# Paged attention in a two-layer decoder step: one more latent page of each unit loaded instead of turned by TensorE

## The chip, the cores and the metric

The kernel runs on one core of one Trainium2 chip. The metric is the device time of one execution in microseconds; the value of a kernel is the median of its runs. The engines are TensorE (PE; its weight loads are listed as PEld), VectorE (DVE), ScalarE (ACT), GpSimd (POOL) and SyncE (SP). A name with a q behind it (ACTq, SPq) is an engine's instruction queue: register work and DMA issues.

## The reference, cut to what matters

One inference step of a small decoder with two layers, for a new prompt of 256 tokens and for 8 samples of 8 new tokens each. The first layer has a gated delta rule mixer, the second latent attention; around each mixer stand two half-step SwiGLU blocks of width 2816. The model width is 1024, everything is float32. What the change touches is the attention of the second layer:

```python
kc  = concatenate([cache_ckv[page_table], c_new])      # latents, 256 wide
kpe = concatenate([cache_kpe[page_table], pe_new])     # rotary keys, 64 wide
s = (q_lat . kc + q_pe . kpe) * scale                   # 8 heads
p = softmax(where(k_pos <= q_pos, s, -inf))
o_lat = p . kc                                          # the same kc as keys and as values
```

A sample has 2048 past tokens in 16 pages of 128 tokens, at places that the page table gives. The latent is both key and value. The scores need a page with the latent's features on the partitions, the values need it with the page's keys on the partitions.

## The kernel before, in words

Weights come in chunks of 1 MB, which ScalarE and VectorE split into a high and a low part (lines 221 to 236); each matmul by weights is three passes of these parts. All of that before and behind the attention is dense work of TensorE. The attention proper starts at 1090 us of the span and ends at 1225 us.

**Units.** The samples are taken in four pairs (NP = 4). A pair's 16 pages go in four quads of QP = 4 pages (NQT = 4), so there are NUN = 16 units; unit i is quad i % 4 of pair i // 4. A unit handles four pages of each of the pair's two samples: the first sample (s = 0) on 64 partitions of the scores, the second (s = 1) on the other 64. Beside it runs one of the 16 pieces of the prompt's own attention (8 heads by 2 query tiles, PU; an even unit has a short piece with one key tile, an odd unit a long one with two). Each iteration n of the loop in attention_pe (line 2308) is, on TensorE:

1. scores_pe(n): 24 matmuls (lines 2240 and 2244) on the feature-major pages in one of three slots;
2. new_values_pe in unit 1, and numerators_pe(n - 1) (line 2256): four transposes of the last unit's exponentials;
3. in units 1, 5, 9 new_scores_pe (lines 2185 to 2187), for the pair's new tokens; then page_plain_pe(n) (line 2267): transposes of pages of the first sample; in units 3, 7, 11 new_transposed_pe (line 2191), in units 4, 8, 12 new_values_pe (line 2195);
4. p_numerators_pe(n) (line 2109): one or two transposes of the prompt's normalized probabilities;
5. values_pe(n - 1) (line 2284): 16 instructions on key-major pages, two for each page, which counts pv_page up by one;
6. p_values_pe(n) and p_scores_pe(n + 1) (lines 2117 and 2098 to 2101), and behind a pair's last values outputs_pe (line 2292).

**Key-major pages.** For the second sample (plain_b) all four come by DMA from cache_c, two by SyncE and two by GpSimd (load_plain, line 2523). For the first sample, pages 2 and 3 come by DMA from ScalarE's queue (plain_c, load_first_plain, line 2512). Pages 0 and 1 are turned by TensorE: page_plain_pe transposes two 128x128 halves of each, out of the feature-major slot, into PSUM bank 6 (C_BANK[0]), and VectorE's copy_plain (line 2409) brings them into plain_a, for all units the same buffer. So it waits until the values of the unit before have read it.

**ScalarE's order** is written out by hand (attention_act, line 2334). In iteration n: the prompt's exponential p_exp_act(n) (line 2124); transposed(n - 1) (line 2348), the copy of the transposed numerators to SBUF for which values_pe waits; numerators(n) (line 2339), the unit's exponential, which waits for VectorE's row maximum; new_exp_act in units 2, 6, 10 (line 2199); p_transposed_act(n) (line 2132), for which p_values_pe waits; p_high_act(n) (line 2139), the copy of the prompt piece's output; then load_first_plain(n + 1); and in units 4, 8, 12 high (line 2353), the copy of a finished pair's output. Each load there is a page number read from SBUF (page_of, line 2500), register work, and the DMA's issue (line 2520).

**VectorE's order** (attention_dve, line 2395): p_mask_dve (lines 2150 to 2155), p_norm_dve (lines 2161 and 2163), which waits for p_exp_act, row_max (lines 2398 to 2403), copy_plain, merge (lines 2417 and 2421), and in units 4, 8, 12 norm, p_low_dve (line 2169) and low (line 2437).

SyncE and GpSimd load the feature-major slots (load_pages, line 2502), each one sample of the pair; the load for unit i waits for c_tr, which page_plain_pe(i - 3) counts up at its end.

Of the kernel before, what the change touches and what calls it, by code (L numbers as in the profile page):

```python
# [27 lines left out]
P = 128  # L28
D_MODEL, SEQ, DEC_B, DEC_S = 1024, 256, 8, 8
FFN_DIM, HEADS, CONV_W = 2816, 8, 4  # L30
PAST, PAGE, KV_LORA, ROPE, NOPE, Q_LORA = 2048, 128, 256, 64, 128, 512
# [18 lines left out]
BASE, NCHUNK = {}, 0  # L50
# [62 lines left out]
def build(nc, io):  # L113
    ctx = ExitStack()
    with ctx:
        def sb(name, shape, dt=F32, where=ctx):
            return where.enter_context(nc.sbuf_tensor(name, shape, dt))


        def sem(name):  # L120
            return ctx.enter_context(nc.semaphore(name))


        raw = [sb(f"raw{i}", [P, CHUNK]) for i in range(2)]
# [10 lines left out]
        ssum = sb("ssum", [P, TOK])  # L135
# [6 lines left out]
        r_pre = sb("r_pre", [P, TOK])  # L142
# [4 lines left out]
        ident = con[:, 0:P]  # L147
# [33 lines left out]
        bank = [psum[:, i, :] for i in range(8)]  # L181
# [1665 lines left out]
        def kv_pool(pool):  # L1847
# [6 lines left out]
        QP = 4  # L1854
# [6 lines left out]
        NTS = 3  # L1861
# [3 lines left out]
        slot = [u.rearrange("p (g s n) -> p g s n", g=QP, s=2) for u in uoff]  # L1865
        qd = marena[:, o_:o_ + 4 * TOK].rearrange("p (t n) -> p t n", t=4)
        o_ += UW
        plain_a = marena[:, o_:o_ + CW_ // 2].rearrange("p (g c) -> p g c", g=QP)
        plain_b = [[raw[BASE["uk"] % 2][:, 1536 + g * KV_LORA:1536 + (g + 1) * KV_LORA] for g in range(2)]
                   + [raw[(BASE["uk"] + 1) % 2][:, 1280 + g * KV_LORA:1280 + (g + 1) * KV_LORA] for g in range(2)],  # L1870
                   [marena[:, o_ + CW_ // 2 + g * KV_LORA:o_ + CW_ // 2 + (g + 1) * KV_LORA] for g in range(QP)]]
        plain_c = [[plain_a[:, 2, :], plain_a[:, 3, :]],
                   [raw[(BASE["uk"] + 1) % 2][:, 1792:1792 + KV_LORA], r_pre[:, 0:KV_LORA]]]
        o_ += CW_
        qpe = marena[:, o_:o_ + HEADS // 2 * TOK].rearrange("p (h t) -> p h t", h=HEADS // 2)
        assert 2 * UW <= H2 and o_ + HEADS * TOK <= AW - H2 - 2 * 2 * HEADS * TOK
# [36 lines left out]
        qland = [qland, sem("plain_landed1")]  # L1913
# [173 lines left out]
        S_BANK, PS_BANK, PP_BANK, PO_BANK, T_BANK, V_BANK, C_BANK = 0, 2, 3, 3, 4, 5, (6, 7)  # L2087
# [130 lines left out]
        def new_acc_dve(dve, p):  # L2218
            dve.wait_ge(n_pv, p + 1)
            dve.tensor_copy(oacc[p], new_bank(KV_LORA)).then_inc(n_acc, 1)  # L2220
# [38 lines left out]
        def page_plain_pe(pe, i):  # L2259
            if i:  # L2260
                pe.wait_ge(c_dve, i)
            if i % NQT == 1 and i > NQT:
                pe.wait_ge(s_lo, 2 * (i // NQT))
            for g in range(2):
                for w in range(2):
                    o = (2 * g + w) * P
                    last = pe.transpose(bank[C_BANK[0]][:, o:o + P], slot[i % NTS][:, g, 0, w * P:(w + 1) * P], ident)
            last.then_inc(c_tr, 1)

        def first_plain(i, g):  # L2270
            return plain_a[:, g, :] if g < 2 else plain_c[i % 2][g - 2]

        def values_pe(pe, i):
            pe.wait_ge(s_trt, i + 1)
            pe.wait_ge(c_dve, i + 1)
            pe.wait_ge(qland[i % 2], 16 * 2 * (i // 2 + 1))
            pe.wait_ge(spland[i % 2], 16 * 2 * (i // 2 + 1))
            pe.wait_ge(ppland[i % 2], 16 * 2 * (i // 2 + 1))
            if i:
                pe.wait_ge(s_o, i)  # L2280
            for g in range(QP):
                for s in range(2):
                    rows = slice(s * NSMP, (s + 1) * NSMP)
                    last = pe.matmul(bank[V_BANK][rows, 0:KV_LORA], pts[:, g, rows], plain_b[i % 2][g] if s else first_plain(i, g),  # L2284
                                     start=(g == 0), stop=(g == QP - 1))
                last.then_inc(pv_page, 1)
# [101 lines left out]
        def olv(a, p, c):  # L2388
            t0 = SEQ + 2 * DEC_S * p
            return a[:, c:2 * HEADS:2, t0:t0 + 2 * DEC_S].rearrange("p h (s t) -> p s h t", s=2)  # L2390

        def obank(c):
            return bank[C_BANK[0]][:, c * P:(c + 1) * P].rearrange("p (s h t) -> p s h t", s=2, h=HEADS)

        def attention_dve(dve):
            def row_max(i):
                dve.wait_ge(s_done, i + 1)
                dve.tensor_reduce(ust(i, 0), psum[:, S_BANK:S_BANK + 2, 0:QP * HP], AX.XY, ALU.max).then_inc(s_mx, 1)
                dve.wait_ge(s_mx, 3 * i + 1)
                old = ust(i - 1, 1) if i % NQT else nst(0, i // NQT)  # L2400
                dve.tensor_tensor(ust(i, 1), ust(i, 0), old, ALU.max).then_inc(s_mx, 1)
                dve.wait_ge(s_mx, 3 * i + 2)
                dve.tensor_scalar(ust(i, 2), ust(i, 1), -SCALE, None, ALU.mult).then_inc(s_mx, 1)

            def copy_plain(i):
                dve.wait_ge(c_tr, i + 1)
                if i:
                    dve.wait_ge(pv_page, QP * (i - 1) + 2)
                dve.tensor_copy(plain_a[:, 0:2, :], bank[C_BANK[0]][:, :].rearrange("p (g c) -> p g c", g=2)).then_inc(c_dve, 1)

            def merge(i):
                p = i // NQT
                dve.wait_ge(s_alpha, i + 1)
                if i % NQT:
                    dve.wait_ge(s_l, i)
                old = ust(i - 1, 5) if i % NQT else nst(2, p)
                dve.scalar_tensor_tensor(out=ust(i, 5), in0=old, scalar=ust(i, 4), in1=ust(i, 3), op0=ALU.mult, op1=ALU.add) \
                   .then_inc(s_l, 1)
                dve.wait_ge(pv_page, QP * (i + 1))
                dve.wait_ge(s_o, i) if i % NQT else dve.wait_ge(n_acc, p + 1)  # L2420
                dve.scalar_tensor_tensor(out=oacc[p], in0=oacc[p], scalar=ust(i, 4), in1=bank[V_BANK][:, 0:KV_LORA],
                                         op0=ALU.mult, op1=ALU.add).then_inc(s_o, 1)

            def norm(p):
                i = NQT * p + NQT - 1
                dve.wait_ge(s_l, i + 1)
                dve.reciprocal(ust(i, 6), ust(i, 5)).then_inc(s_nrm, 1)
                dve.wait_ge(s_nrm, 2 * p + 1)
                dve.wait_ge(s_o, i + 1)
                if p:  # L2430
                    dve.wait_ge(s_ot, p)
                dve.tensor_scalar(osb, oacc[p], ust(i, 6), None, ALU.mult).then_inc(s_nrm, 1)

            def low(p):
                for c in range(2):
                    dve.wait_ge(s_hi, 2 * p + 2)
                    dve.tensor_tensor(olv(ol_lo, p, c), obank(c), olv(ol_hi, p, c).bitcast(F32), ALU.subtract).then_inc(s_lo, 1)

            pack_dve(dve)
            for n in range(NUN):  # L2440
                p_mask_dve(dve, n)
                if n < NU - 1:
                    p_norm_dve(dve, n)
                if n == 0:
                    new_mask_dve(dve, 0)
                row_max(n)
                if n == 1:
                    new_acc_dve(dve, 0)
                copy_plain(n)
                if n > 0:  # L2450
                    merge(n - 1)
                    if n % NQT == 0:
                        norm(n // NQT - 1)
                if pair_of(n, 3):
                    new_mask_dve(dve, pair_of(n, 3))
                if pair_of(n, 0):
                    new_acc_dve(dve, pair_of(n, 0))
                if n < NU - 1:
                    p_low_dve(dve, n)
                else:  # L2460
                    p_norm_dve(dve, n)
                if n > 0 and n % NQT == 0:
                    low(n // NQT - 1)
            merge(NUN - 1)
            norm(NP - 1)
            p_low_dve(dve, NU - 1)
            low(NP - 1)
            split_lo(dve, BASE["uk"] + 2)
# [16 lines left out]
        def pack_dve(dve):  # L2485
            dve.wait_ge(qlat0_ready, latent_act(HEADS - 1))
            dve.wait_ge(qlat_ready, latent_dve(HEADS - 1))
            dve.tensor_copy(qpk_dst(1), qlat_smp(1)).then_inc(q_packed, 1)
            dve.wait_ge(qpe_ready, HEADS // 2)
            for q in range(2):  # L2490
                dve.tensor_copy(qpk_dst(2)[0:ROPE, :, q:HEADS:2, :], qpe_smp(q)).then_inc(q_packed, 1)
# [20 lines left out]
        def load_first_plain(act, i):  # L2512
            p, q = i // NQT, i % NQT
            if i >= 2:
                act.wait_ge(pv_page, QP * (i - 1))
            else:
                act.wait_ge(lo_ready, BASE["uk"] + 1 + i)
            for g in (2, 3):
                n = page_of(act, 2 * p, QP * q + g)
                act.dma_start(plain_c[i % 2][g - 2], io["cache_c"][bass.ds(n, 1), :, :].rearrange("a p c -> p (a c)")) \  # L2520
                   .then_inc(qland[i % 2], 16)

        def load_plain(eng, f, land, i):
# [354 lines left out]
```

## Time and profile before

| What | us |
|---|---|
| Median of 3 runs | 1510.95 (1510.17 to 1512.41) |
| The profiled execution | 1515.13 |
| Its span | 1513.5 |
| TensorE busy | 1463.5 (97%) |
| VectorE busy | 908.8 (60%) |
| ScalarE busy | 746.0 (49%) |
| GpSimd busy | 144.1 (10%) |

The granted clock of TensorE is full (0.992 in the mean) over the execution. In the page's part 6, the loads of the attention are 160 KB each for feature-major pages (cache_t) and 128 KB each for key-major pages (cache_c).

How to read it: a busy time adds up instructions of an engine, and does not count register work, semaphores and the issuing of DMAs. In a timeline a line is one instruction or several of a kind (x4), with its start from the start of the span, its length, and in brackets the idle time of the engine before it and what ended it. The chain that ended last follows the execution back from its end: each piece is the work that released the next. In it a matmul's piece is the time by which it advances the chain; the same matmul's own length is longer, since matmuls overlap.

### The profile page before, as it was taken

How to read it: one execution, taken by the hardware profiler on the slowest of the kernel's cores; microseconds unless marked ns; L12 is line 12 of the kernel's file. 1: busy time of each engine (PE TensorE's matmuls, PEld its weight loads, DVE VectorE, ACT ScalarE, POOL GpSimd, SP SyncE). 2: the span in 40 equal slices, each digit the busy share in tenths (PEclk: the TensorE clock that was granted, in tenths of full speed). 3: DMA queues.
4: the chain of work that ended last, by engine and by line, in shares of the span. 5: the costliest groups of instructions: out<-in, count | busy, mean ns of one | idle time of the engine just before them, and what ended most of it. 6: DMA issues, size and time to landing. Idle time of an engine off the chain costs nothing.

```text
span 1513.5 us, 29771 instructions
## 1 busy us (share of the span) xinstructions
PE 1463.5 (97%) x11042; PEld 1371.8 (91%) x11042; DVE 908.8 (60%) x1512; ACT 746.0 (49%) x1200; POOL 144.1 (10%) x209
## 2 busy tenths in 40 slices
PE   8999999999989899999999999999999999999997
PEld 8999998999877889999989999997866688999996
DVE  5655536979967586564377555337655547655534
ACT  5555425678454365554255555325533345555432
POOL 0111000000100001110001111000143300111000
PEclk9999999999999999999999999999999999999998
DMA  6444343333321224434425434443588742443441
GB/s 219 156 150 154 139 148 110 141 138 140 122 97 54 115 103 155 162 139 141 164 84 180 164 139 149 152 143 109 185 265 248 235 161 94 170 153 140 145 159 62
DMA packets 50563, 222.62 MB, mean 147 GB/s; under 512 B 6625, under 2 KB 23138, under 8 KB 28338
## 3 DMA queue, kind: packets, MB, share of 16 engines
q1 hardware_dynamic: 39682, 192.70, 36.0%
q0 software_dynamic: 6192, 24.64, 4.9%
q10 hardware_dynamic: 4608, 4.20, 0.9%
q8 instruction: 51, 0.84, 0.2%
q14 instruction: 30, 0.25, 0.1%
HBM read 214.74 MB, written 6.77 MB: 146 GB/s over the span
## 4 chain that ended last, share of the span: by engine, by line
PE 87%; DVE 8%; ACT 2%; issue 2%; DMA 1%; ACTq 0%; SPq 0%; DVEq 0%
PE psum L246 15%; PE psum L247 15%; PE psum L251 15%; PE psum L325 8%; PE psum L327 8%; PE psum L326 8%; PE psum L2284 2%; PE psum L2240 2%; DVE x L390 1%; PE psum L2117 1%; DVE y L386 1%; DMA raw<-wts 1%; DVE w_lo L234 1%; DVE h_lo L432 1%; PE psum L1281 1%
## 5 line engine op out<-in xcount | busy, mean ns | idle before, releaser
L234 DVE TENSOR_TENSOR w_lo<-raw,w_hi 128x2048 fp32r<-128x2048 f32 x163 | 377.8, 2318 | 316.6 <-ACT w_hi L227 316.3
L227 ACT ACTIVATE w_hi<-raw 128x2048 fp32r<-128x2048 f32 x158 | 302.7, 1916 | 365.0 <-PE psum L327 221.8
L246 PE MATMUL psum<-h_hi,w_hi 128*128 128x320 f32 x1536 | 458.0, 311 | 3.1 <-ACT w_hi L227 1.8
L247 PE MATMUL psum<-h_lo,w_hi 128*128 128x320 f32 x1536 | 456.2, 310 | 0.0
L246 PEld LDWEIGHTS psum<-h_hi,w_hi 128*128 128x128 f32 x1536 | 290.3, 189 | 4.7 <-ACT w_hi L227 2.1
L247 PEld LDWEIGHTS psum<-h_lo,w_hi 128*128 128x128 f32 x1536 | 290.4, 189 | 0.5
L251 PE MATMUL psum<-h_hi,w_lo 128*128 128x320 f32 x1536 | 257.2, 309 | 0.0
L251 PEld LDWEIGHTS psum<-h_hi,w_lo 128*128 128x128 f32 x1536 | 234.0, 188 | 0.2
L325 PE MATMUL psum<-hid_hi,w_hi 128*128 (+1 forms) x704 | 217.8, 309 | 4.1 <-DVE f_g L618 4.1
L327 PE MATMUL psum<-hid_hi,w_lo 128*128 (+1 forms) x704 | 217.5, 309 | 0.0
L326 PE MATMUL psum<-hid_lo,w_hi 128*128 (+1 forms) x704 | 217.4, 309 | 0.0
L645 POOL TENSOR_TENSOR f_gu<-f_g,f_u 128x320 f32<-128x320 f32 x88 | 78.5, 892 | 642.3 <-DVE f_u L619 642.3
L325 PEld LDWEIGHTS psum<-hid_hi,w_hi 128*128 128x128 f32 x704 | 132.2, 188 | 5.0 <-DVE f_g L618 5.0
L326 PEld LDWEIGHTS psum<-hid_lo,w_hi 128*128 128x128 f32 x704 | 132.2, 188 | 0.0
L327 PEld LDWEIGHTS psum<-hid_hi,w_lo 128*128 128x128 f32 x704 | 132.2, 188 | 0.0
L599 ACT ACTIVATE hid_hi<-f_h 128x320 f32 x88 | 41.5, 472 | 132.3 <-DVE f_h L623 132.3
L618 DVE TENSOR_TENSOR f_g<-psum,r_pre 128x320 f32<-128x320 f32 x88 | 43.2, 491 | 85.9 <-PE psum L251 79.7
L626 DVE TENSOR_TENSOR hid_lo<-f_h,hid_hi 128x320 f32 x88 | 43.3, 492 | 67.0 <-ACT hid_hi L599 67.0
L595 ACT ACTIVATE f_e<-f_e,onec 128x320 f32<-128x320 f32 x88 | 49.6, 564 | 2.8
L623 DVE TENSOR_TENSOR f_h<-f_gu,f_e 128x320 f32<-128x320 f32 x88 | 42.6, 484 | 0.8 <-POOL f_gu L645 0.8
L597 ACT ACTIVATE f_e<-f_e 128x320 f32<-128x320 f32 x88 | 41.6, 473 | 2.8
L619 DVE TENSOR_TENSOR f_u<-psum,r_pre 128x320 f32<-128x320 f32 x88 | 42.3, 481 | 0.0
(406 smaller groups left out, 1930.0 us busy)
## 6 DMA issues: line engine op xcount, KB each, us to landing
raw<-wts SPq DMA_DIRECT2D x164, 1024.0 KB, 4.8
h_plain<-cache_t POOLq DMA_DIRECT2D x44, 160.0 KB, 3.6
h_plain<-cache_t SPq DMA_DIRECT2D x44, 160.0 KB, 3.5
arena<-s POOLq DMA_DIRECT2D x4, 1024.0 KB, 6.3
sgs<-arena POOLq DMA_DIRECT2D x4, 1024.0 KB, 4.2
marena<-cache_t POOLq DMA_DIRECT2D x20, 160.0 KB, 3.8
marena<-cache_t SPq DMA_DIRECT2D x20, 160.0 KB, 3.4
raw<-wts SPq DMA_DIRECT2D x4, 512.0 KB, 8.6
```

What stands on the lines that cost most here:

```text
L227: act.activation(w_hi[c0 % 2][:, :], raw[c0 % 2][:, :], ACT.Copy).then_inc(hi_ready, 1)
L234: eng.tensor_tensor(w_lo[c0 % 2][:, :], raw[c0 % 2][:, :], w_hi[c0 % 2][:, :].bitcast(F32), ALU.subtract).then_inc(lo_ready, 1)
L246: pe.matmul(outs[n], wtile(w_hi, c0, n * K + k), src_hi(k), start=(k == 0), stop=False)
L247: pe.matmul(outs[n], wtile(w_hi, c0, n * K + k), src_lo(k), start=False, stop=False)
L251: last = pe.matmul(outs[n], wtile(w_lo, c0, n * K + k), src_hi(k), start=False, stop=(k == K - 1))
L325: pe.matmul(o, wtile(w_hi, c0, 2 * m + kk), s_hi, start=(start and kk == 0), stop=False)
L326: pe.matmul(o, wtile(w_hi, c0, 2 * m + kk), s_lo, start=False, stop=False)
L327: last = pe.matmul(o, wtile(w_lo, c0, 2 * m + kk), s_hi, start=False, stop=(stop and kk == 1))
L595: act.activation(f_e[i][:, :], f_e[i][:, :], ACT.Ln, bias=onec[:, :]).then_inc(d_ready, 1)
L618: dve.tensor_tensor(f_g[i][:, :], bank[2 * i][:, 0:TOK], r_pre[:, :], ALU.mult).then_inc(g_ready, 1)
L626: dve.tensor_tensor(one(hid_lo), f_h[i][:, :], one(hid_hi).bitcast(F32), ALU.subtract) \
L645: pool.tensor_tensor(f_gu[i][:, :], f_g[i][:, :], f_u[i][:, :], ALU.mult).then_inc(gu_ready, 1)
```

## The change

Page 1 of the first sample is loaded by ScalarE's queue, as pages 2 and 3 are, and page_plain_pe turns page 0 only. In even units it lands in plain_a[:, 1], in odd units in ssum, a row-sum buffer that nothing uses during the attention. The copy to SBUF takes half the columns and waits for one page of the unit before instead of two; values_pe waits for three loads of ScalarE's queue.

```diff
-        plain_c = [[plain_a[:, 2, :], plain_a[:, 3, :]],
-                   [raw[(BASE["uk"] + 1) % 2][:, 1792:1792 + KV_LORA], r_pre[:, 0:KV_LORA]]]
+        plain_c = [[plain_a[:, 1, :], plain_a[:, 2, :], plain_a[:, 3, :]],
+                   [ssum[:, 0:KV_LORA], raw[(BASE["uk"] + 1) % 2][:, 1792:1792 + KV_LORA], r_pre[:, 0:KV_LORA]]]
...
-            for g in range(2):
-                for w in range(2):
-                    o = (2 * g + w) * P
-                    last = pe.transpose(bank[C_BANK[0]][:, o:o + P], slot[i % NTS][:, g, 0, w * P:(w + 1) * P], ident)
+            for w in range(2):
+                last = pe.transpose(bank[C_BANK[0]][:, w * P:(w + 1) * P], slot[i % NTS][:, 0, 0, w * P:(w + 1) * P], ident)
             last.then_inc(c_tr, 1)
 
         def first_plain(i, g):
-            return plain_a[:, g, :] if g < 2 else plain_c[i % 2][g - 2]
+            return plain_a[:, 0, :] if g == 0 else plain_c[i % 2][g - 1]
...
-            pe.wait_ge(qland[i % 2], 16 * 2 * (i // 2 + 1))
+            pe.wait_ge(qland[i % 2], 16 * 3 * (i // 2 + 1))
...
-                    dve.wait_ge(pv_page, QP * (i - 1) + 2)
-                dve.tensor_copy(plain_a[:, 0:2, :], bank[C_BANK[0]][:, :].rearrange("p (g c) -> p g c", g=2)).then_inc(c_dve, 1)
+                    dve.wait_ge(pv_page, QP * (i - 1) + 1)
+                dve.tensor_copy(plain_a[:, 0, :], bank[C_BANK[0]][:, 0:KV_LORA]).then_inc(c_dve, 1)
...
-            for g in (2, 3):
+            for g in (1, 2, 3):
                 n = page_of(act, 2 * p, QP * q + g)
-                act.dma_start(plain_c[i % 2][g - 2], io["cache_c"][bass.ds(n, 1), :, :].rearrange("a p c -> p (a c)")) \
+                act.dma_start(plain_c[i % 2][g - 1], io["cache_c"][bass.ds(n, 1), :, :].rearrange("a p c -> p (a c)")) \
                    .then_inc(qland[i % 2], 16)
```

## Rows read from the trace of the kernel before

**Rows 1.** the page, parts 1 and 4: busy times, chain by engine
```profile
PE 1463.5 (97%) x11042; PEld 1371.8 (91%) x11042; DVE 908.8 (60%) x1512; ACT 746.0 (49%) x1200; POOL 144.1 (10%) x209
...
PE 87%; DVE 8%; ACT 2%; issue 2%; DMA 1%; ACTq 0%; SPq 0%; DVEq 0%
```

**Rows 2.** busy us of PE, PEld, DVE, ACT, POOL; clock; DMA share; GB/s
```profile
1100.00:1200.00 100.00, 98.56 (x777) 63.45 (x773) 53.84 (x175) 34.77 (x111) 40.84 (x77) 1.00 0.86 265
```

**Rows 3.** groups by line, 1093 to 1225 us: transposes and copy
```profile
L2409 DVE COPY marena<-psum 128x512 f32<-128x512 f32 x16 | 11.1, 692 | 23.4 <-PE psum L2284 22.2 <-PE psum L2267 1.2
...
L2267 PE MATMUL psum<-con,h_plain 128*128 128x128 f32 x44 | 6.8, 276 | 0.0
```

**Rows 4.** timeline of ScalarE, units 0 to 1; start us, us, what
```profile
1097.76 0.38 ACT L2139 ACTIVATE ol_hi<-psum 128x256 fp32r<-128x256 f32 x1 [0.18 <-PE psum L2117]
1098.43 0.34 ACTq L2520 DMA_DIRECT2D raw<-cache_c  x1
1099.47 0.34 ACTq L2520 DMA_DIRECT2D r_pre<-cache_c  x1
1099.86 0.51 ACT L2124 ACTIVATE y<-y,ssx 128x256 f32<-128x256 f32 x1 [1.72 <-DVE ssx L2155]
```

**Rows 5.** timeline of ScalarE, end of unit 5 to the start of unit 7
```profile
1140.59 1.40 ACTq L2520 DMA_DIRECT2D marena<-cache_c  x2
1142.04 0.40 ACT L2124 ACTIVATE y<-y,ssx 128x128 f32<-128x128 f32 x1 [1.74 <-DVE ssx L2155]
...
1145.59 0.26 ACT L2132 ACTIVATE y<-psum 128x128 f32<-128x128 f32 x1
1147.11 0.38 ACT L2139 ACTIVATE ol_hi<-psum 128x256 fp32r<-128x256 f32 x1 [1.27 <-PE psum L2117]
...
1149.78 0.51 ACT L2124 ACTIVATE y<-y,ssx 128x256 f32<-128x256 f32 x1 [2.28 <-DVE ssx L2155]
```

**Rows 6.** timeline of VectorE, unit 6: normalization and row maximum
```profile
1142.77 0.32 DVE L2163 TENSOR_SCALAR y<-y,ssx 128x128 f32<-128x128 f32 x1
1143.28 0.69 DVE L2398 TENSOR_REDUCE lnv<-psum 128x1 f32<-128x512 f32 x1 [0.20 <-PE psum L2244]
```

**Rows 7.** chain that ended last, units 6, 7; start us, us, what
```profile
1143.84 0.60 ACT raw L2348
1144.49 1.95 PE psum L2284 x16
1146.44 0.64 PE psum L2117 x4
...
1151.63 0.44 PE psum L2267 x4
...
1152.39 1.88 PE psum L2284 x16
```

**Rows 8.** timeline of ScalarE, units 8 to 9, and unit 13's exponential
```profile
1164.87 0.35 ACTq L2520 DMA_DIRECT2D r_pre<-cache_c  x1
1165.27 0.45 ACT L2353 ACTIVATE ol_hi<-psum 128x128 fp32r<-128x128 f32 x2 [1.73 <-PE psum L2292]
1167.31 0.51 ACT L2124 ACTIVATE y<-y,ssx 128x256 f32<-128x256 f32 x1 [1.59 <-DVE ssx L2155]
...
1200.00 0.51 ACT L2124 ACTIVATE y<-y,ssx 128x256 f32<-128x256 f32 x1 [1.59 <-DVE ssx L2155]
```

**Rows 9.** chain that ended last, units 9 and 13: prompt transposes and values
```profile
1169.60 1.88 PE psum L2284 x16
...
1201.24 0.44 PE psum L2109 x2
1201.68 1.88 PE psum L2284 x16
```

**Rows 10.** ScalarE's register loads (ns min/median/max) and page landings
```profile
L2500 ACTq TENSOR_LOAD <-pages x32: 272/277/461, 1089.4 to 1212.9; - x32
...
DMA to landing us min/median/max: 2.1/4.2/5.0
```

## The prediction

> **What bounds the kernel now.** I read the page first, for the engine that sets the end, then a stretch inside the attention, then the chain of waits, and last ScalarE's own timeline. The page gives TensorE 97% of the span and 87% of the chain that ended last [rows 1]. In the hundred microseconds inside the attention it is busy 98.56 of 100 at the full granted clock, with VectorE at 54, ScalarE at 35 and the DMA engines at a share of 0.86 [rows 2]. That invites the reading "take work off TensorE, ScalarE has room". But issuing DMAs is not counted as busy, so ScalarE's 35 understates it. Its timeline [rows 4] shows what it does between two units: it copies the prompt head's output (1097.76), issues the two page loads (1098.43, 1099.47), and starts the next prompt softmax exponential (1099.86) just 0.05 us after the second load's issue ends (1099.81). The queue is full there, though the engine looks idle. So the change takes from the engine that bounds most of the stretch and gives to a queue that bounds the rest; the answer has to be made unit by unit. I number the 16 units as the loop does.
>
> **What is removed.** Two of four transposes in each unit, 32 in all, with their weight loads. One lasts 0.276 us [rows 3], but they are pipelined: four advance the chain by 0.44 us [rows 7], so two are worth 0.22 us where TensorE is the last to be ready. VectorE's copy out of PSUM (0.692 us, 16 times) becomes half as wide, and may start one page earlier. VectorE waits 22.2 us for the values matmuls ahead of 15 of these 16 copies [rows 3], and the merge that follows still needs all four pages, so I cost this at nothing; it is bounded by 0 and by half of 0.692 us a unit.
>
> **What is added.** A third value load, register work and DMA issue on ScalarE. The two present ones start 1.04 us apart [rows 4]; the third adds 1.04 us to every gap between the output copy and the next exponential. The transfer is one more 128 KB page beside a unit's 14 page loads (eight of 160 KB, six of 128 KB); it is issued a unit before the values that use it. For the last unit the third issue falls about 2.8 us after the output copy of unit 14, and its values start some 5.9 us later; a landing takes 2.1 to 5.0 us, median 4.2 [rows 10]. This is hidden, with the least cover (0.9 us at the longest landing) in that last unit. SP and GpSimd issue what they issued; their next key-major loads are released by the end of the transposes, 0.22 us earlier, and compete for nothing new except the page itself.
>
> **Where the 1.04 us goes.** Queued behind it on ScalarE are the exponential, the copy of the transposed numerators, the unit's own exponential and the copy of the prompt's transposed probabilities; TensorE waits for all of these.
>
> Unit 1: the exponential starts as soon as the queue lets it [rows 4], and the chain runs from it through VectorE's normalization and row maximum into TensorE. Full price: +1.04. Units 0 and 1 give back 0.22 each: together **+0.60**.
>
> Units 2, 6, 10 (unit 6 shown): TensorE's values now wait for ScalarE's copy (1143.84) and start 0.65 us later, at 1144.49 [rows 7]. All four transposes are hidden under that copy: nothing is gained. The exponential stands 0.05 us behind the loads (end 1141.99) and slides from 1142.04 to 1143.08 [rows 5]. VectorE's normalization ended at 1143.09, 1.05 us behind the exponential, and the row maximum could start at 1143.28, with the scores [rows 6]; now it starts at about 1144.1, +0.8. From the row maximum to the probabilities' copy the work is back to back (1143.28 to 1145.59, ending 1145.85) [rows 5, 6]; its end moves to 1146.65, and TensorE wants it at 1146.44 [rows 7]. So +0.3 here, and as much in unit 10. Unit 2 begins behind a slow register load (they reach 0.461 us against a median of 0.277 [rows 10]), so 0.5. Together **+1.1**.
>
> Units 3, 7, 11 (unit 7 shown): the exponential waits for VectorE, at 1149.78, while the two issues end near 1149.17, 2.06 us behind the output copy at 1147.11 [rows 5], the distance that [rows 4] show. It slides by only 0.45 and finds cover. Values would start 0.22 earlier than 1152.39, at 1152.17, but ScalarE's copy holds them to 0.65 after the end of the numerators' transposes at 1151.66, that is 1152.31 [rows 7]: gain 0.08 each, **-0.24**.
>
> Units 4, 8, 12: the copy of the new tokens' values lies between; TensorE is last throughout and the late exponential is hidden. **-0.66**.
>
> Units 5, 9 (unit 9 shown): ScalarE must still copy the finished pair's output (1165.27, 0.05 us behind the second load), VectorE works on that, and the exponential follows at 1167.31 [rows 8]. It moves to 1168.35. In unit 13 the prompt transposes follow the exponential by 1.24 us and the values follow these by 0.44 [rows 8, 9], so the values start at 1170.03 instead of 1169.60 [rows 8]: +0.43, and the gain is swallowed. Unit 5 has a slow register load before it and 0.3 less cover: 0.73. Together **+1.16**.
>
> Unit 13: here the exponential at 1200.00 already sets the values at 1201.68 [rows 8, 9]. Full price: **+1.04**, nothing gained. Units 14 and 15: transposes under ScalarE's copy, the rest covered: 0.
>
> Sum: 0.60 + 1.1 - 0.24 - 0.66 + 1.16 + 1.04 = **+3.0 us**. The profiled execution took 1515.13 us (span 1513.5), so it would take 1518.1. It stands 4.2 us above the median of the runs, 1510.95; I add the same 3.0 to the median: **1514.0 us**. Everything behind the attention is bound by TensorE and moves with it. 0.2%, about what a measurement of this kernel can tell from no change, is 3.02 us: my forecast lies on that line, a hair on the slow side.
>
> The price of one more load is the number all this hangs on, and the rows bound it by 0.9 (one chain of register load, 0.28, address work and the 0.34 of the issue cannot be much shorter than the pitch they show) and, with a slow register load in each, 1.04 + 0.46 - 0.28 = 1.22; in seven exposed units that is -1 and +1.3 us about the sum. The Trainium skill, DMA: Bandwidth & Descriptors, Latency and other measured facts, gives a floor of about 0.6 us for a register load from SBUF. The trace doesn't agree: 0.277 us. By the page the issue would cost 0.33 us more, in the seven exposed units together 2.3 us, 1516.3 in all; I go by the row.
>
> **Rivals.**
> (a) *ScalarE's queue has room and only TensorE's saving shows; the other side.* One mechanism: the late exponential is absorbed by waits that exist anyway. ScalarE shows 35 busy of 100 [rows 2], and in three units of sixteen it does wait for VectorE. Against it: the 0.05 us gap recurs ahead of 11 of the 15 later exponentials (directly, or through the output copy), and in units 1 and 13 the chain itself runs through the load issues. It decides if the added issue costs below about 0.4 us. Then the gain is 0.22 in units 0, 1, 4, 5, 8, 9, 12 and 0.08 in three: 1.8 us, 1509.2; with every transpose counted, 32 x 0.11 = 3.5 us, 1507.4. Chance 0.15. The Trainium skill, same page, Issuing engines are not separate DMA queues, says that the sequencer's time to initiate a DMA is usually small relative to the DMA; by that rule this rival would hold. The row shows 1.04 us of issue beside 4.2 us to landing, a quarter.
> (b) *The delay is exposed nearly everywhere*, because a unit that has lost its cover hands its lateness on. Eleven exponentials by 1.04 and three by 0.45 make 12.8 us, less 0.66: 1523. For it: several covers are under 0.1 us in my working. Against: units 4, 8, 12 have over half a microsecond. A half-way case is 1518. Chance of 1517.5 or more: 0.1.
> (c) *The third page lands late and TensorE's values wait for it.* The DMA engines' share is already 0.86 [rows 2]; one page more is 128 of 2,048 KB, 6%, and makes it 0.91. It decides if landings go beyond 5.9 us; a late last page by 1 us gives 1515. Chance 0.05.
> (d) My sum within its bounds, 1512 to 1517.5: 0.7.
>
> **The numbers.** The likeliest is (d), 1514.0. Range 1510.0 to 1518.0: it leaves out most of (a) and the far part of (b). Slower by over 0.2%: the upper half of (d), all of (b), most of (c), 0.5. Within 0.2%: the lower half of (d) and part of (a), 0.42. Faster: the end of (a) where all transposes count, 0.08.
>
> **What would show it.** In the changed profile: three load issues about 1.04 us apart behind each output copy; the exponential 3.15 us instead of 2.1 us behind that copy in 11 units; TensorE idle for VectorE's normalization in units 5, 9, 13 and for the probabilities' copy in 2, 6, 10; 32 transposes left; VectorE's copy near 0.4 us; the attention, from the first scores to the output projection's first matmul, about 3 us longer. I am wrong if the third issue costs clearly less than 1 us, if units 4, 8 and 12 don't shorten by 0.22, or if the time moves outside the attention.

## The result and the profile after

The changed kernel took 1518.68 us in the median of 7 runs (1515.49 to 1522.82), the kernel before 1512.95 us in the runs beside it; the ratio is 1.0033 with a 95% interval of 1.0017 to 1.0048. On the 1512.95 that is 5.0 us more, between 2.6 and 7.3. A second series gave 1.0037 (1.0023 to 1.0052). I forecast +3.0: the sign is right, the size is on the low side. The kernel before measured 2.0 us more in this series than the 1510.95 that the forecast started from; on 1510.95 the two ratios give 1515.9 and 1516.5, inside my range of 1510.0 to 1518.0.

From the page, parts 1, 3 and 4 (q10 is ScalarE's DMA queue):

```profile
PE 1459.5 (96%) x11010; PEld 1365.9 (90%) x11010; DVE 903.7 (60%) x1512; ACT 745.8 (49%) x1200; POOL 144.1 (10%) x209
...
q10 hardware_dynamic: 6912, 6.29, 1.3%
...
PE 85%; DVE 8%; ACT 2%; issue 2%; ACTq 1%; DMA 1%; SPq 0%; DVEq 0%
```

TensorE is 4.0 us less busy than in [rows 1] and carries 85% of the chain instead of 87%. The kernel lost work on its busiest engine and became slower: that is the whole case in one line. ScalarE's queue moved 6912 packets where it had moved 4608.

A whole execution is a poor ruler here. In the profile of before the attention's first matmul comes at 1090.31 us, in this one at 1085.83 and in a second profile of before at 1092.80, though nothing there was changed: ahead of the attention the granted clock fell four times in the first profile of before, twice in this one and seven times in the second of before. So I measure inside the profile, from the first prompt scores (L2098) to the first matmul behind the attention (L2544 before, L2542 after), and call it the stretch: 1090.31 to 1225.14 before, **134.83 us**; 1085.83 to 1226.81 after, **140.98 us**. That is +6.15.

Unit by unit, from the starts of ScalarE's copy L2139, each counted from the start of the stretch; a figure is what the unit adds to the difference against before:

| Unit | forecast | after | after, second profile |
|---|---|---|---|
| 0 | -0.22 | -0.22 | -0.23 |
| 1 | +0.82 | **+3.73** | **+3.94** |
| 2 | +0.5 | +0.47 | +0.23 |
| 3, 7, 11, each | -0.08 | 0.00 | 0.00 |
| 4, 8, 12, each | -0.22 | -0.22 | -0.22 |
| 5 | +0.73 | +0.47 | +0.48 |
| 6 | +0.3 | +0.63 | +0.23 |
| 9 | +0.43 | +0.44 | +0.46 |
| 10 | +0.3 | +0.24 | +0.51 |
| 13 | +1.04 | +1.06 | +1.05 |
| 14, 15 | 0 | 0 | 0 |

Fifteen units are within 0.35 us of the working, most within 0.05. One unit holds nearly all of the miss.

ScalarE's timeline from unit 0 to unit 1 of the changed kernel answers to [rows 4]:

```profile
1093.06 0.38 ACT L2139 ACTIVATE ol_hi<-psum 128x256 fp32r<-128x256 f32 x1 [0.18 <-PE psum L2117]
1093.73 0.34 ACTq L2518 DMA_DIRECT2D ssum<-cache_c  x1
1094.78 0.34 ACTq L2518 DMA_DIRECT2D raw<-cache_c  x1
1095.81 0.34 ACTq L2518 DMA_DIRECT2D r_pre<-cache_c  x1
1096.21 0.51 ACT L2124 ACTIVATE y<-y,ssx 128x256 f32<-128x256 f32 x1 [2.76 <-issue]
```

Three issues 1.05 and 1.03 us apart, and the exponential 3.15 us behind the copy instead of 2.10. Before, the same exponential stood 0.05 us behind the second issue; now it stands 0.05 behind the third. What TensorE waits for in the attention (waited for, total us, times, longest):

```profile
PE psum L2109 <- DVE y L2163: 3.6, 6, 1.4
PE psum L2185 <- DVE sq L2220: 2.1, 1, 2.1
...
PE psum L2117 <- ACT y L2132: 0.6, 3, 0.2
PE psum L2282 <- ACT raw L2346: 0.5, 1, 0.5
```

Before, TensorE had three such waits of its matmuls in the attention, 1.7 us together. Now it waits six times for VectorE's normalization (L2163), in units 5, 9 and 13 as forecast, in 2 and 6, where ScalarE had a slow register load or issue besides, and in 15 as before; and three times for the prompt's probabilities (L2132), in units 2, 6 and 10, as forecast. The wait in L2185, 1.0 us before, is 2.1. It is the one in unit 1, and the next view says what it did. Busy us of PE, PEld, DVE, ACT, POOL, then the granted clock, the DMA engines' share and GB/s, in pieces around it:

```profile
1096.00:1097.00 1.00, 0.71 (x5) 0.42 (x4) 0.16 (x1) 0.79 (x3) 0.53 (x1) 1.00 0.96 324
1097.00:1098.00 1.00, 0.00 (x0) 0.00 (x0) 0.95 (x3) 0.34 (x1) 0.54 (x1) 1.00 0.82 259
1098.00:1099.00 1.00, 0.24 (x1) 0.24 (x2) 0.64 (x3) 0.59 (x2) 0.54 (x1) 0.64 1.04 317
1099.00:1101.00 2.00, 2.00 (x9) 1.76 (x10) 0.00 (x0) 0.37 (x3) 0.54 (x1) 0.50 0.99 332
...
1103.00:1105.00 2.00, 2.00 (x12) 0.75 (x8) 0.25 (x2) 0.00 (x0) 0.61 (x2) 0.50 0.81 238
1105.00:1107.00 2.00, 2.00 (x16) 1.71 (x14) 1.31 (x5) 0.38 (x1) 1.00 (x2) 0.97 0.82 201
```

TensorE does nothing for two microseconds, and when it starts again the granted clock is at half, 1.2 of 2.4 GHz, until shortly after 1105. The chain shows what that costs; its pieces for the values of unit 1 and for the end of unit 2's wait:

```profile
1101.53 3.61 PE psum L2282 x16
...
1112.65 0.33 ACT r_post L2199 x2
1113.19 0.71 PE psum L2117 x4
```

The values take 3.61 us where they took 1.88 in this unit before and take 1.88 to 1.97 in the others now. (The other two pieces are unit 2's: ScalarE's exponential of the new tokens, L2199, stands ahead of its copy of the probabilities, and TensorE's L2117 waits for that copy.)

The chain in unit 6's loads and in unit 13:

```profile
1141.38 0.73 ACTq L2518
...
1202.91 0.44 PE psum L2109 x2
1203.35 1.88 PE psum L2282 x16
```

Unit 6 lost 0.63 where it lost 0.23 in the second profile: one DMA issue took 0.73 us instead of 0.34. Unit 13 is [rows 9] moved by the third issue. And VectorE's copy, which was 692 ns in [rows 3]:

```profile
L2407 DVE COPY marena<-psum 128x256 f32<-128x256 f32 x16 | 6.8, 425 | 10.0 <-PE psum L2282 9.0 <-PE psum L2265 1.0
```

Half as wide, 425 ns, and as forecast it bought nothing: no unit gained clearly more than the 0.22 of the transposes.

### The profile page after: what moved, and what is told of

Same layout as the page of the kernel before. It is cut to its first block, busy times and chain, and to the rows that moved or that the text cites. A ratio compares the mean times of both kernels' runs of the same rounds, so it can differ in the third digit from the quotient of the medians.

```text
span 1515.1 us, 29803 instructions
## 1 busy us (share of the span) xinstructions
PE 1459.5 (96%) x11010; PEld 1365.9 (90%) x11010; DVE 903.7 (60%) x1512; ACT 745.8 (49%) x1200; POOL 144.1 (10%) x209
## 3 DMA queue, kind: packets, MB, share of 16 engines
q10 hardware_dynamic: 6912, 6.29, 1.3%
## 4 chain that ended last, share of the span: by engine, by line
PE 85%; DVE 8%; ACT 2%; issue 2%; ACTq 1%; DMA 1%; SPq 0%; DVEq 0%
PE psum L246 15%; PE psum L247 15%; PE psum L251 15%; PE psum L325 8%; PE psum L327 8%; PE psum L326 8%; PE psum L2282 2%; DVE x L390 1%; PE psum L2240 1%; PE psum L2117 1%; DVE y L386 1%; DVE w_lo L234 1%; DMA raw<-wts 1%; DVE h_lo L432 1%; ACTq L2518 1%
```

## The experiments

Two theories were on the table. **Queue and clock**: ScalarE's time to issue is the price, exposed as in the working, and the idle gap of 2.05 us in unit 1 lets the clock fall, 2.9 us more. **Others**: the clock falls by chance; the transfer, not the issue, costs; ScalarE has room.

### fill_gap and fill_fit: put matmuls into the gap

```diff
                 numerators_pe(pe, n - 1)
+                if n == 1:
+                    keep_busy(pe, 4, V_BANK, 448)
                 if pair_of(n, 3):
```

> The changed kernel with four matmuls of 448 columns into a bank that is free then, put into the gap of unit 1 in which TensorE waits about 2 us for VectorE. Nothing else is altered. The stretch is the attention, from the first prompt scores to the first matmul of the output projection of the values: 134.8 us before, 141.0 us after. Theory (queue and clock): TensorE's granted clock fell to the lower level because it stood idle for 2.05 us there; with the gap filled the clock stays full, unit 1 costs 0.8 instead of 3.7 us, and the stretch is 138.1. Rival (the slow matmuls of unit 1 have another cause, as contention with the page loads): the clock or the matmuls stay slow and the stretch stays at 141.

Measured: stretch 138.24, clock full throughout it, ratio 1.0006 (0.9992 to 1.0021). Unit 1 cost 1.51, not 0.8: four such matmuls last 3.17 us, more than the gap, and delay the work behind them. So fill_fit, with 2 in the place of 4:

> The changed kernel with two matmuls of 448 columns (some 1.5 us) in the gap of unit 1 where TensorE waits 2.05 us, instead of the four that overfilled it by about 0.7 us. Theory (in the changed kernel the clock falls in that gap in every execution): the clock stays full there, unit 1 costs 0.83 us, the attention stretch is 138.0 against 141.0, and the mean granted clock of the runs is 0.994 or more in most, where the changed kernel's runs were all at 0.993 or less. Rival (the clock falls by chance, whatever stands in the gap): the runs' clocks are spread as those of the changed kernel.

TensorE's timeline in the gap of fill_fit (each matmul stands there as two records), and busy times with the granted clock in two stretches of 4 us:

```profile
1096.83 1.67 PE L499 MATMUL psum<-con,ones 128*128 128x448 f32 x4
1099.04 0.43 PE L2185 MATMUL psum<-ckvT,raw 128*128 128x64 f32 x2 [0.54 <-DVE sq L2220]
```

```profile
1096.00:1100.00 4.00, 3.46 (x17) 1.90 (x16) 1.76 (x6) 2.10 (x6) 1.90 (x4) 1.00 0.90 284
1100.00:1104.00 4.00, 4.00 (x34) 2.89 (x33) 1.54 (x6) 0.73 (x2) 1.33 (x3) 1.00 0.86 272
```

The fill (L499) leaves a wait of 0.54 us, and the clock stays at 1.00. Unit 1 cost 0.82, the forecast's figure, and the stretch is 138.08: +3.25 on before, against the forecast's +3.0. That is the change's cost with a full clock, some 0.5 of it from unit 6, where one DMA issue again was slow (0.80 us; the unit cost 0.73, and 0.24 in fill_gap). The second half of the expectation missed: the runs' mean clocks were 0.989 to 0.997, five of eight under 0.994, and the median 1516.74, ratio 1.0026 (1.0008 to 1.0044). Falls elsewhere in the execution can hide one fall's absence in eight runs. The two ratios, 1.0006 and 1.0026, belong to stretches 0.16 us apart, so whole times of so few runs don't settle it; the profiles do.

### load_only: the cost without the saving

```diff
-            for g in (2, 3):
+            for g in (1, 2, 3):
                 n = page_of(act, 2 * p, QP * q + g)
-                act.dma_start(plain_c[i % 2][g - 2], io["cache_c"][bass.ds(n, 1), :, :].rearrange("a p c -> p (a c)")) \
+                dst = plain_c[i % 2][g - 2] if g > 1 else spare[:, i % 2 * KV_LORA:(i % 2 + 1) * KV_LORA]
+                act.dma_start(dst, io["cache_c"][bass.ds(n, 1), :, :].rearrange("a p c -> p (a c)")) \
```

> The kernel before, all four transposes kept, with a third page load on ScalarE's queue into a buffer of its own that nothing reads, but for which the values wait as in the change. Theory (queue and clock): all of the cost and none of the saving. Unit 1 again loses about 4 us with the clock's fall, units 2, 6, 10 about 0.3 to 0.6, 5 and 9 about 0.5, 13 about 1.05, and nothing is given back in units 0, 4, 8, 12: the stretch goes from 134.8 to 142. Rival (ScalarE's queue has room, and the change loses by something else, such as the buffers or the copy): within 1 us of 134.8.

Measured: stretch 140.28, +5.45; ratio 1.0033 (1.0021 to 1.0045). Units 0, 3, 4, 7, 8, 11, 12, 14 cost 0.00, units 2, 6, 10 0.24 to 0.30, 5 and 9 0.48 and 0.45, unit 13 1.06. Unit 1 cost 2.65, not 4. Busy times in its gap and behind it:

```profile
1103.00:1104.00 1.00, 0.00 (x0) 0.00 (x0) 0.96 (x3) 0.17 (x1) 0.51 (x1) 1.00 0.90 270
...
1105.00:1106.00 1.00, 1.00 (x7) 0.86 (x6) 0.00 (x0) 0.19 (x2) 0.54 (x1) 0.77 0.94 344
1106.00:1108.00 2.00, 2.00 (x12) 1.29 (x12) 0.00 (x0) 0.38 (x1) 0.13 (x1) 0.50 0.72 240
```

The clock fell again, here only after TensorE had started again at 1104.58, and it was back after some 3.5 us instead of 7. So the same gap has a price that varies: 1.6 us here, which is unit 1's 2.65 less the 1.04 of the delay. ScalarE has no room: the rival falls. All of this loss is made by a load that nothing reads.

### no_load: the saving without the cost

```diff
-            for g in (1, 2, 3):
+            for g in (2, 3):
                 n = page_of(act, 2 * p, QP * q + g)
...
-            return plain_a[:, 0, :] if g == 0 else plain_c[i % 2][g - 1]
+            return plain_a[:, 0, :] if g == 0 else plain_c[i % 2][max(g, 2) - 1]
```

> The changed kernel without the third load: two transposes in a unit, two loads; page 1's values are taken from page 2's buffer, so the part of the values that belongs to page 1 is left out and page 2 counts twice. Theory: the saving alone, 0.22 us in units 0, 1, 4, 5, 8, 9, 12 and at most 0.08 in 3, 7, 11, none in the units where TensorE waits for ScalarE's copy: the stretch is 133.0 to 133.3. Rival (every transpose counts): 32 times 0.11, 131.3. Second rival (nothing is saved, another wait takes over): 134.8.

Measured: stretch 136.40, and the ratio 0.9987 (0.9973 to 1.0000). By the stretch none of the three expectations. The units say why: 0, 4, 5, 8, 9 and 12 save 0.21 or 0.22 each and the others 0.00 to 0.02, as the theory has it, but unit 1 costs 2.93. TensorE's wait there, and the clock behind it:

```profile
PE psum L2185 <- DVE sq L2220: 1.0, 1, 1.0
```

```profile
1096.00:1100.00 4.00, 2.99 (x23) 1.62 (x20) 2.15 (x8) 2.16 (x6) 1.84 (x4) 0.96 0.94 276
1100.00:1104.00 4.00, 4.00 (x18) 2.52 (x20) 0.55 (x2) 0.38 (x1) 1.88 (x4) 0.50 0.90 290
1104.00:1108.00 4.00, 4.00 (x24) 2.83 (x22) 1.60 (x6) 0.38 (x1) 1.64 (x4) 0.69 0.86 250
```

The wait is the 1.0 us of before, and the clock fell nonetheless. In two profiles of before, and in sp_third, the same wait left the clock alone. Without the fall unit 1 would, by the other units, have saved 0.22, and the stretch would be 133.25; sp_third, the next run, shows just that.

### sp_third: the same bytes from another queue

ScalarE loads pages 2 and 3 again; load_plain gets, behind its own two loads:

```diff
+            if f == 0:
+                n = page_of(eng, 2 * p, QP * q + 1)
+                eng.dma_start(plain_c[i % 2][0], io["cache_c"][bass.ds(n, 1), :, :].rearrange("a p c -> p (a c)")) \
+                   .then_inc(land[i % 2], 16)
```

> The changed kernel, but the load of page 1 is issued by SyncE's queue behind its two key-major loads instead of by ScalarE's. The same bytes move and the same buffers are used. Theory (the price is ScalarE's time to issue): the stretch is that of the saving alone, 133.0 to 133.3, and the whole kernel 1.5 us faster than before. Rival (the price is the transfer, the DMA engines' share or the landing): the stretch stays near 141. SyncE's queue takes seven issues of 1.09 us in a unit of some 8.3 us, so it could begin to be late; then the feature-major pages land late and the scores wait.

Measured: stretch 133.25, -1.58; ratio 0.9997 (0.9982 to 1.0011). Every other unit is as in no_load, and unit 1 saves 0.21. The transfer costs nothing; the rival falls. What SyncE's queue waited for in the attention:

```profile
SPq L2498 <- PE psum L2265: 13.9, 1, 13.9
```

Before, it had waited 12 times for the transposes, 30.0 us together and 15.3 the longest. Only the long wait is left, 13.9 us: SyncE's queue is nearly full with seven issues, but no wait of TensorE in the attention ended with a page's landing. The whole-kernel gain of 1.5 us is smaller than what 11 runs can show.

### fill_before, hoist_after, hoist_fill

fill_before puts one such matmul into the gap of the kernel before.

> The kernel before with one matmul of 448 columns (0.76 us) in its own gap of 1.01 us in unit 1. Theory (that shorter gap lets the clock fall in a part of the executions, as it did in the profile of the kernel without the third load, but not in the profile of before): the attention stretch is 134.8 in the profile, none of the runs shows the fall, the lowest clocks become rarer, and the median is 1 to 2 us under the kernel before. Rival (a gap of 1 us does nothing): same median and same spread of clocks.

Measured: stretch 134.90; median 1511.24, ratio 0.9993 (0.9980 to 1.0006). The median is 1.0 us under before's, the near edge of the expectation, and not distinguishable from before. No profile of before shows a fall in this gap, so this profile says nothing either: inconclusive.

hoist_after reads ScalarE's page numbers ahead of the copy:

```diff
+                ns = first_pages(act, n + 1) if n < NUN - 1 else None
                 if n < NU - 1:
                     p_high_act(act, n)
...
-                    load_first_plain(act, n + 1)
+                    load_first_plain(act, n + 1, ns)
```

> The changed kernel, but ScalarE reads the three page numbers ahead of the copy of the prompt's output, where it waits for TensorE anyway; only the three issues stay between that copy and the exponential. Theory (the price is the time ScalarE's queue takes there, most of it the register loads): an issue without its register load takes 0.4 us, three take 1.3 instead of 3.1, less than the two of before, 2.1. The exponential is no longer late in any unit, all of the saving shows and unit 13 gains about 0.3 more: stretch 132.4 (132.0 to 133.0). Rival (the issue itself is what takes the time): above 137.

Measured: stretch 137.33; ratio 1.0005 (0.9991 to 1.0019). A miss by 5 us, most of it in units 0 and 1. ScalarE's timeline there:

```profile
1095.84 0.38 ACT L2139 ACTIVATE ol_hi<-psum 128x256 fp32r<-128x256 f32 x1 [1.35 <-issue]
1096.00 0.35 ACTq L2522 DMA_DIRECT2D ssum<-cache_c  x1
1096.51 0.34 ACTq L2522 DMA_DIRECT2D raw<-cache_c  x1
1097.00 0.41 ACTq L2522 DMA_DIRECT2D r_pre<-cache_c  x1
1097.76 0.51 ACT L2124 ACTIVATE y<-y,ssx 128x256 f32<-128x256 f32 x1 [1.53 <-DVE ssx L2155]
```

Three issues now end 1.57 us behind the start of the copy, near what was expected: they are 0.5 us apart, so half of the 1.04 is the register load with its address work. But the copy itself, at 1095.84, is 1.17 us late: in unit 0 ScalarE has no idle time ahead of it, and the register loads only moved from behind the copy to before it. Against before, unit 0 cost 0.95 and the gap in unit 1 grew to 2.0 us; the clock fell to half there once more, unit 1 cost 2.54. Unit 2 cost 0.35 because a single DMA issue ahead of it, at 1108.50, took 2.08 us. In the units from 3 on the theory holds: 0.00 or -0.22 in every one, unit 13 included.

hoist_fill adds one matmul to the gap:

> hoist_after with one matmul of 448 columns in unit 1's gap. Theory: stretch as hoist_after within 0.3, full clock in unit 1 in the runs, median 2 to 3.5 us under the kernel before. Rival (the fill is in the way, the gap being too short by then): longer than hoist_after by up to 0.7.

Measured: stretch 134.04, the clock full; ratio 0.9998 (0.9984 to 1.0012). The clock is kept, with a wait of 1.24 us left behind the fill, and unit 1 gives -0.40, but unit 0's 0.95 stays, which the expectation had not known of. The median, 1512.12 beside 1512.27 of before, misses its 2 to 3.5 us.

### sp_hoist_fill: what the runs point to, and two repeats

> The version the runs so far point to: page 1's load on SyncE's queue, ScalarE's two page numbers read ahead of the copy of the prompt's output from unit 1 on (not in unit 0, where hoist_after showed that ScalarE has no time there), one matmul of 448 columns in unit 1's gap. Theory: the stretch is that of sp_third, 133.25, less 0.2 to 0.3 in unit 13: 133.0; unit 1 costs nothing and its clock stays full; the kernel is 1.5 to 3 us faster than before and 5 or more faster than the changed one. Rival (SyncE's seven issues in a unit are late with some page): some unit longer than before.

Measured: median 1509.71, ratio **0.9985 (0.9974 to 0.9996)**, the only version whose interval lies wholly under the kernel before, by 2.3 us in 1512.5 (0.6 to 3.9); among nine versions, one interval at this distance could also be luck, and the profile's stretch gives 1.8. The changed kernel beside it (after_again, below) took 8.4 us more. Stretch 133.05. Unit 13 saves 0.22 where sp_third saved 0.02. ScalarE's timeline behind unit 13's copy:

```profile
1203.45 0.38 ACT L2139 ACTIVATE ol_hi<-psum 128x256 fp32r<-128x256 f32 x1 [1.30 <-PE psum L2117]
1203.59 1.03 ACTq L2524 DMA_DIRECT2D marena<-cache_c  x2
1205.15 0.40 ACT L2124 ACTIVATE y<-y,ssx 128x128 f32<-128x128 f32 x1 [1.31 <-DVE ssx L2155]
```

The two issues now end at 1204.62, and half a microsecond is free ahead of the exponential, where before there was 0.05.

> The changed kernel once more, word for word, for a second profile and a ratio beside the version above. Theory (a wait of 2 us in unit 1 lets the clock fall there as a rule): the stretch is 141.0 again within 0.3, with the granted clock at half for some 6 us in unit 1. Rival (the fall there was chance): the stretch is 138.1, unit 1 costs 0.8. The ratio to before is 1.002 to 1.005 either way.

Measured: stretch 140.82, the clock at half for nearly 7 us in unit 1; ratio 1.0037 (1.0023 to 1.0052). The figures are in the table above.

> The kernel before once more, word for word, for a second profile. Its wait in unit 1 is 1.01 us. If such a wait lets the clock fall by chance, as it did in the profile of no_load and not in those of before and sp_third, the stretch is 134.8 or about 137.8; elsewhere in the stretch every unit is as before within 0.1. If the shorter wait never does it in this kernel: 134.8.

Measured: stretch 134.79, every unit within 0.03 of the first profile. The clock didn't fall in the stretch. It did fall in seven places ahead of it, and the execution took 1517.59, which shows how little one execution's total says.

## Why the prediction was right in its sign and low in its size

**Removed.** 0.22 us where TensorE is last: right to a hundredth, in units 4, 8, 12 of every run with two transposes, in unit 0 of all of these but the two with the hoist there, and in 5 and 9 of no_load and sp_third. The 0.08 in units 3, 7, 11 was 0.00: matmuls that start after a wait advance the chain by 1.95 us instead of 1.88, and that gave it back.

**Added.** 1.04 us an issue: 1.03 to 1.05. The Trainium skill's floor for a register load (DMA: Bandwidth & Descriptors, Latency and other measured facts) would have made it 1.37 or so (an estimate, 1.04 plus the prediction's 0.33), and the trace again doesn't agree: the issues keep their pitch in the changed kernel, and hoist_after's 0.5 us pitch leaves some 0.55 for the register load with its address work. The transfer at nothing: right, by sp_third.

**Where it goes.** Right within 0.35 us in each unit but one, and the sum of the others is right to 0.25 us. (One sign was miscounted: the exponential stood 2.1 us behind the copy ahead of eight units, not 11; ahead of units 5, 9 and 13 it stood 4.2 to 4.5 behind and now stands 5.2.) The step that failed is "Unit 1: ... Full price: +1.04". The delay had its price, +0.82 net in fill_fit, but I costed TensorE's wait only as time. It grew from 1.01 to 2.05 us, and towards its end the granted clock fell to half. Unit 1's new-token scores, transposes and values, 3.5 us of the chain at the full clock, then took 6.4: 2.9 us more in the first profile (3.73 - 0.82), 3.1 in the second, 1.6 in load_only. My prediction read the clock row, "full", and used every duration at that clock; it didn't ask whether the longer wait would keep it. Neither a term of the sum nor a rival has this loss. That the time still lies inside the range is the range's width, 8 us, and luck, not foresight.

**Is the fall caused by the change?** Four profiles have the wait at 2.0 to 2.1 us (after, twice, load_only and hoist_after): it fell in all four. Four have it at 1.0 us (before, twice, sp_third, no_load): it fell in one. Five have matmuls in the gap: it fell in none, and three of them (fill_gap, fill_fit, hoist_fill) are kernels whose gap would be 2.0 us without the fill. hoist_fill kept its full clock with a wait of 1.24 us left, so not the wait's length alone decides. That the fill prevents it and that the longer wait makes it likelier fits all thirteen; that 2 us always do it is not shown by four. The mean clock of whole executions points the same way, less sharply: it was 0.994 or more in one of 16 of the changed kernel and none of 10 of load_only, in 10 of 12 of fill_gap but only 3 of 8 of fill_fit, and in 16 of 35 of before beside the first experiments. How often the shorter wait does it is open, since only the profiled execution of a series shows the place.

**The total.** 3.25 at full clock plus 2.9 for the fall is the stretch's 6.15; the ratios give 5.0 (2.6 to 7.3) and, on 1512.49, 5.6 (3.5 to 7.9), whose intervals hold it. The first holds 3.25 too: that the fall is part of the loss rests on the profiles.

**Rivals.** (a), that ScalarE has room, fell with load_only: the same ratio as the change, 1.0033, from a load nobody reads. The Trainium skill says in DMA: Bandwidth & Descriptors, Issuing engines are not separate DMA queues, that the sequencer's time to initiate a DMA is usually small relative to the DMA. It is not small here: an issue holds ScalarE's queue for 1.04 us beside 4.0 us to landing in the changed kernel, and moving it alone from ScalarE to SyncE is worth 7.7 us of stretch (140.98 to 133.25, the fall of the clock with it). (b), exposed nearly everywhere, whose half-way case was +7, came near the stretch's size but not for its reason: units 3, 4, 7, 8, 11 and 12 hid the delay. (c), the late page, fell with sp_third.

## What to carry to other kernels

An engine that the page calls half idle can be full at one place of its order: DMA issues and register loads aren't counted as busy, so look for the instruction that starts right behind the last issue. Put a new issue on the queue whose next instruction nobody waits for (SyncE's here), and read its page number where the engine waits anyway. When an edit lengthens a wait of TensorE, price the wait and then the work behind it at half the clock, and try a matmul or two in the gap.

## What the runs showed of the hardware that I had not expected

The granted clock fell to half behind a wait of TensorE of only 1.0 us (no_load) to 2.1 us, though TensorE had worked for some 11 us without a wait, and stayed there for 3.5 to 7 us. In load_only and no_load it fell only after TensorE had started again. The same wait of 1.0 us, in the same place, left it full in three other profiles, one of which (sp_third) has the same work of TensorE before it as no_load.

A DMA issue on ScalarE usually takes 0.34 us, but single ones took 0.59 to 0.80 us (after, after_again, fill_fit, sp_third) and once 2.08 us (hoist_after). Where the queue was full such a straggler cost 0.2 to 0.5 us: in units 2 and 6 of the first profile of the changed kernel, in unit 10 of the second and in unit 6 of fill_fit.
